# Attention masks and decay rows ahead of the wait for the keys, first row maxima ahead of the last level's queries, and the mixer turned by tile

## The chip, the cores and the metric

The kernel runs on one core of one Trainium2 chip. Its engines work side by side, each through its own queue in order: TensorE (PE in the profile; PEld is its weight load), VectorE (DVE), ScalarE (ACT), GpSimd (POOL) and SyncE (SP), which issues most of the transfers. They wait for each other by semaphores. The metric is the device time of one execution in microseconds; less is better.

## What is computed

A decoder trunk of two layers on 256 tokens of width 1024. In each layer one input projection feeds three groups of heads: a gated linear recurrence (HGRN2), an mLSTM, and a forgetting attention. Their outputs go through one output projection, and a channel mixer follows: dense in layer 0, eight experts of which each token takes two in layer 1. The parts that matter here, cut from the reference:

```python
def block(args):                      # forgetting attention, blocks of 128 queries, 8 heads
    qb, cb, bi = args
    qpos = bi * Q_BLOCK + jnp.arange(Q_BLOCK)
    s = (jnp.einsum('bhqd,bhkd->bhqk', qb, k).astype(f32) * scale
         + cb[..., None] - c[:, :, None, :])       # c = cumsum(log f): the decay rows
    s = jnp.where(kpos[None, :] <= qpos[:, None], s, -jnp.inf)
    p = jax.nn.softmax(s, axis=-1)
    return jnp.einsum('bhqk,bhkd->bhqd', p.astype(v.dtype), v)
...
for l in range(DEPTH):
    h = rmsnorm(x, attn_norm[l])
    ... = jnp.split(h @ w_in[l], split_idx, axis=-1)
    o_hg = hgrn2_mixer(...); o_ml = mlstm_mixer(...); o_fx = fox_mixer(...)
    mix = jnp.concatenate([o_hg, o_ml, o_fx], axis=-1)
    x = x + mix @ w_out[l]
    h = rmsnorm(x, ffn_norm[l])
    x = x + (swiglu(h, ...) if l % 2 == 0 else moe_swiglu(h, ...))
return rmsnorm(x, final_norm)
```

## The kernel before

**Products in halves.** A float32 operand is split in a high part (a cast, by ACT) and a low part (the rest, by DVE); three matmuls make one product (the helper `three`, L1664 to L1666). So each half slab of weights costs ACT one cast (`weights_high`, L887) and DVE one subtraction (`weights_low`, L1188) before PE can use it.

**The step loop.** The input projection is cut in 14 half slabs. PE, DVE and ACT each run a loop over 12 steps k with the same shape. In step k PE projects half slab k + 2 (`project`), and in the middle of it (`between`) multiplies one level of the HGRN2 scores (`level(l, k - 1)`, 9 levels) and turns attention weights. After the projection of step 3 PE spreads a row to 128 partitions with four products of 4 rows (L1896, eight matmuls in the profile). After that of steps 7, 8 and 9 it makes the attention scores of three groups (`attn_scores(l, 0..2)`); after that of steps 8 to 10 it turns the weights of a group (`attn_turn`), and from step 9 on it multiplies them with the values (`attn_apply`).

**Attention scores.** For each of two banks: one matmul that writes the causal mask (L1802), then per head one that adds the decay rows (L1807, from the tile `CT`), then per head queries by keys (L1813). `CT` holds the decay rows' high part, cast by ACT (L986, semaphore `s_cth`), and their low part, by DVE (L1393, `s_ctl`). Group 0 first waits for the mLSTM exponents to have left the banks (`s_e0`), for eight evacuated half slabs (`s_pe`; the keys are the last two of them), and for `s_ctl`. Groups 1 and 2 wait for the exponentials of the group before (`s_ex`), which read the same banks.

**DVE's step.** In step k: the level's queries (`level_queries`, L1229 and for level 8 L1232), the differences of the next level (`level_difference`, L1216 to L1222), in step 7 the decay rows' low part, in steps 8 to 10 the row maxima of a group (`attn_max`: two reductions L1257 and a negation L1261), then the copy of the last level's scores (`level_copy`), the attention weights (`attn_weights`), and the low part of half slab k + 4. ACT's step: the level's decays (L967, L969), the exponentials (`attn_exp`, L915), the copy of turned weights (L924), the evacuation (L871 for the values) and the cast of half slab k + 4. POOL makes the level's keys (L775).

**The end of the mixers.** After the loop PE makes the sums of the mLSTM and HGRN2 heads. Then come the output projection's rows that belong to attention (`for i in (NHALF, NHALF + 1)`, 48 matmuls of 512 columns), then the turns of the other heads' output `OM`, tile 0 into bank 3 and tile 1 into bank 0 (L1970), each after its wait for `s_og`. ACT copies each turned tile (L1014, `s_me`), DVE makes its low part (`mix_low`, L1199, `s_ml`), and PE goes on with the rows of these heads (L1977, L1978, L1983).

Of the kernel before, what the change touches and what calls it, by code (L numbers as in the profile page):

```python
# [21 lines left out]
P = 128  # L22
F32 = mybir.dt.float32
F32R = mybir.dt.float32r
I32 = mybir.dt.int32
ALU = mybir.AluOpType
# [8 lines left out]
def bass_hybrid_trunk_kernel(nc, x, attn_norm, w_in, hgrn_lb, hgrn_norm, mlstm_conv, mlstm_b_i,  # L35
# [3 lines left out]
    _, SEQ, D = x.shape  # L39
    DEPTH = w_in.shape[0]  # L40
    T = SEQ // P
# [5 lines left out]
    NFH = FW // DH  # L47
# [20 lines left out]
    NHALF = 2 * len(SLABS)  # L68
# [47 lines left out]
    with ExitStack() as ctx:  # L116
# [6 lines left out]
        ps = [ctx.enter_context(nc.psum_tensor(f"bank{i}", [P, BANK], F32)) for i in range(8)]  # L123
# [31 lines left out]
        OM = last_slot[:, 0:1024].rearrange("p (t h d) -> p t h d", t=T, h=2 * NH)  # L155
# [8 lines left out]
        CT = nc.alloc_sbuf_tensor_at("CT", [P, SEQ], F32R, offset=shared + 4 * decay_at)  # L164
# [21 lines left out]
        ident = sb("ident", [P, P])  # L186
# [122 lines left out]
        s_pe = sem("projection_evacuated")  # L309
# [16 lines left out]
        s_cth = sem("decay_rows_high")  # L326
        s_ctl = sem("decay_rows_low")
# [23 lines left out]
        s_og = sem("heads_gated")  # L351
        s_mt = sem("mix_turned")
# [795 lines left out]
        def _(dve):  # L1148
# [151 lines left out]
            for l in range(DEPTH):  # L1300
# [60 lines left out]
                level_difference(l, 1)  # L1361

                for k in range(STEPS):
                    if 1 <= k < LEVELS:
                        level_queries(l, k)
                        if k + 1 < LEVELS:
                            level_difference(l, k + 1)
                    if k == 1:
                        dve.wait_ge(s_aT, l + 1)
                        for t in range(T):  # L1370
                            v = slice(t * P, (t + 1) * P)
                            if t:
                                dve.wait_ge(s_g, T * l + t)
                            dve.tensor_tensor_scan(gT[:, v], ps[7][0:NH, 64 + t * P:64 + (t + 1) * P], MM[0:NH, P:2 * P],
                                                   0.0 if t == 0 else gT[:, t * P - 1:t * P], ALU.max, ALU.max).then_inc(s_g, 1)
                    if k == 4:
                        dve.wait_ge(s_gi, 2 * l + 1)
                        dve.wait_ge(s_a, 2 * l + 2)
                        dve.tensor_tensor(bb[:, :, :], bb[:, :, :], ps[7][:, 400:408].rearrange("p (t h) -> p t h", t=T),
                                          ALU.add).then_inc(s_m, 1)  # L1380
                    if k == 6:

                        dve.wait_ge(s_gi, 2 * l + 2)
                        dve.wait_ge(s_cv, 4 * CK * (l + 1))
                        for h in range(NH):
                            g = ps[4 + h // 2][:, (h % 2) * SEQ:(h % 2 + 1) * SEQ]
                            dve.scalar_tensor_tensor(out=E[:, h // 2, h % 2, 0:SEQ], in0=g, scalar=aa[:, 0, h:h + 1],
                                                     in1=MM[:, :], op0=ALU.add, op1=ALU.min).then_inc(s_e0, 1)
                            dve.scalar_tensor_tensor(out=E[:, h // 2, h % 2, SEQ:], in0=g[:, P:], scalar=aa[:, 1, h:h + 1],
                                                     in1=MM[:, 0:P], op0=ALU.add, op1=ALU.min).then_inc(s_e0, 1)  # L1390
                    if k == 7:
                        dve.wait_ge(s_cth, l + 1)
                        dve.tensor_tensor(CT[32:32 + NFH, :], ps[7][0:NFH, 0:SEQ], CT[0:NFH, :].bitcast(F32),  # L1393
                                          ALU.subtract).then_inc(s_ctl, 1)
                    if 8 <= k < 11:
                        attn_max(l, k - 8)
                    if l == 0 and k == 0:
                        dve.wait_ge(s_prT, 1)
                        dve.tensor_copy(PC[:, :], ps[6][:, 0:NROWS]).then_inc(s_pc, 1)
                        dve.wait_ge(s_pc, 1)  # L1400
                        dve.tensor_tensor(LB[:, 0, :], PCl[:, 1, :], PCl[:, 0, :], ALU.subtract).then_inc(s_lb, 1)
                    if l == 0 and k == 7:
                        dve.wait_ge(s_rw, 16)
                        dve.wait_ge(s_pc, 1)
                        dve.tensor_tensor(RW[:, :, :], RW[:, :, :], bc(PC[:, GAINS0:NROWS].unsqueeze(2), [P, KD, NE]),
                                          ALU.mult).then_inc(s_rwg, 1)
                    if l == 0 and k == 2:
                        gate_weights_low(1)
                        lower_bound()
                    if k == 0:  # L1410
                        level_copy(l, 0)
                    if 2 <= k <= LEVELS:
                        level_copy(l, k - 1)
                    if 2 <= k < 2 + CK:
                        convolve(l, k - 2)
                    if 8 <= k < 11:
                        attn_weights(l, k - 8)
                    if k + 4 <= NHALF:
                        weights_low(l, k + 4)
                    if k >= 9:  # L1420
                        attn_out_low(l, k - 9)

                dve.wait_ge(s_e, l + 1)
                for r, b0, v in ((0, 2, slice(0, SEQ)), (1, 4, slice(SEQ, SEQ + P))):
                    dve.wait_ge(s_qk, 2 * l + r + 1)
                    n = v.stop - v.start
# [234 lines left out]
        def _(pe):  # L1661
# [129 lines left out]
            def attn_scores(l, g):  # L1791

                if g == 0:
                    pe.wait_ge(s_e0, 8 * (l + 1))
                    pe.wait_ge(s_pe, NHALF * l + 8)
                    pe.wait_ge(s_ctl, l + 1)
                else:
                    pe.wait_ge(s_ex, 3 * l + g)
                heads = range(NFH) if g == 0 else range(4 * (g - 1), 4 * g)
                n, w, qt = (4, P, 0) if g == 0 else (2, SEQ, 1)  # L1800
                for p in range(2):
                    pe.matmul(ps[4 + p][:, :].rearrange("q (c s) -> q c s", c=n), identr[:, :],  # L1802
                              NM[:, 2 * P - w:].unsqueeze(1).to_broadcast([P, n, w]), start=True, stop=False,
                              skip_group_check=True)
                for h in heads:
                    at = (h // 2 * w) % BANK
                    pe.matmul(ps[4 + h % 2][:, at:at + w], PICK[:, h:h + 1].to_broadcast([P, P]), CT[:, 0:w],  # L1807
                              start=False, stop=False, skip_group_check=True)
                for h in heads:
                    p, c = h % 2, h // 2  # L1810
                    r = slice(DH * p, DH * p + DH)
                    at = (c * w) % BANK
                    ins = pe.matmul(ps[4 + p][:, at:at + w], FQ[r, c, qt * P:(qt + 1) * P], FK[r, c, 0:w],  # L1813
                                    start=False, stop=True, skip_group_check=True)
                ins.then_inc(s_S, 1)
# [42 lines left out]
            for l in range(DEPTH):  # L1858
# [16 lines left out]
                for k in range(STEPS):  # L1875
                    if k == 1:
                        pe.wait_ge(s_a, 2 * l + 2)
                        for t in range(T):
                            ins = pe.transpose(ps[7][0:NH, 64 + t * P:64 + (t + 1) * P], aa[:, t, :], ident[:, :])
# [9 lines left out]
                    if k == 3:  # L1889

                        pe.wait_ge(s_g, T * (l + 1))
                        for t in range(T):
                            ins = pe.transpose(ps[7][:, 400 + t * NH:400 + (t + 1) * NH], gT[:, t * P:(t + 1) * P], ident[0:NH, 0:NH])
# [20 lines left out]
                for h in range(NH):  # L1914
                    c, p = h // 2, h % 2
# [6 lines left out]
                for h in range(NH):  # L1922
                    c, p = h // 2, h % 2
# [5 lines left out]
                for h in range(NH):  # L1929
                    c, p = h // 2, h % 2  # L1930
# [18 lines left out]
                def out_rows(i):  # L1949

                    pe.wait_ge(s_wil, NCAST * l + i + 1)
                    return cast_places(i)

                for i in (NHALF, NHALF + 1):
                    wh, wl = out_rows(i)
                    for n in range(2):
                        for t in range(T):
                            for r in range(2):
                                k, v = 4 + 2 * (i - NHALF) + r, slice(t * P, (t + 1) * P)
                                w = slice(r * D + n * BANK, r * D + (n + 1) * BANK)  # L1960
                                ins = three(ps[4 + 2 * n + t][:, :], mxh[:, k, v], mxl[:, k, v], wh[:, w], wl[:, w],
                                            k == 4, False)
                    if i == NHALF:
                        ins.then_inc(s_wk, 1)
                for t in range(T):
                    pe.wait_ge(s_og, T * l + t + 1)
                    b = ps[3] if t == 0 else ps[0]
                    om = OM[:, t, :, :].rearrange("p h d -> p (h d)")
                    for c in range(4):
                        ins = pe.transpose(b[:, c * P:(c + 1) * P], om[:, c * P:(c + 1) * P], ident[:, :])  # L1970
                    ins.then_inc(s_mt, 1)
                wa, wb = out_rows(NHALF + 2), cast_places(NHALF + 3)
                pe.wait_ge(s_me, T * l + 1)
                for n in range(2):
# [216 lines left out]
```

## Time and profile before

| what | value |
|---|---|
| median of 3 runs | 1481.24 us (1481.13 to 1481.51) |
| the profiled execution | 1481.19 us, span 1479.4 us |
| busy PE / DVE / ACT / POOL | 1460.5 / 1176.3 / 971.2 / 122.6 us |
| mean granted clock of PE | 0.994 |
| read from HBM, written | 435.36 MB, 14.16 MB |

Times of rows are microseconds from the span's start. In a timeline row stand the start, the length of the group, the engine, the line, the operation, the tile written and the tiles read, the shapes, how many (x2), and in brackets how long the engine was idle before it and what ended that. Several instructions of one line in a row are merged to one group, and matmuls overlap, so a group's start plus its length can lie behind the next start. Layer 0's mixers take about the first 150 us, its dense mixer goes to about 350, layer 1's mixers to about 504, and the experts fill the rest.

### The profile page before, as it was taken

Reading aid. Unit: us, or ns where it says so; the run is one execution under the profiler, and the core shown is the slowest. Engines: PE = TensorE matmul, PEld = TensorE weight load, DVE = VectorE, ACT = ScalarE, POOL = GpSimd, SP = SyncE. Lnnn points to the kernel's source line nnn. Section 1 sums busy time; section 2 is a strip of 40 time slices with the busy share of each in tenths; the row PEclk is TensorE's granted clock in tenths of the full one; section 3 lists DMA queues with packets and bytes.
Section 4 is the critical chain, followed back from the end, with each engine's and each line's share of the span. In section 5 each row is a group of like instructions: output and inputs, shape, how many; then the busy total and the mean of one; then the engine's idle time right before and its main releaser. Section 6 shows DMA issues by size and latency. Waiting matters only on the chain.

```text
span 1479.4 us, 20868 instructions
## 1 busy us (share of the span) xinstructions
PE 1460.5 (99%) x7859; PEld 1240.9 (84%) x7859; DVE 1176.3 (80%) x931; ACT 971.2 (66%) x892; POOL 122.6 (8%) x137
## 2 busy tenths in 40 slices
PE   9999999999999999999999999999999999999997
PEld 8978899998988888888888888888888888888885
DVE  5776555455885788888888888888888888888897
ACT  4455444444646477777777777777777777777775
POOL 5212000000120280000000000000000000000200
PEclk9999999999999999999999999999999999999999
DMA  8633966553342499999999999999999999999993
GB/s 253 222 115 114 315 231 231 190 171 129 115 142 87 171 342 393 396 391 394 380 357 397 389 369 386 385 370 384 388 376 373 394 375 368 394 379 363 399 394 150
DMA packets 210284, 450.27 MB, mean 304 GB/s; under 512 B 12940, under 2 KB 37048, under 8 KB 210232
## 3 DMA queue, kind: packets, MB, share of 16 engines
q1 hardware_dynamic: 209080, 445.35, 82.5%
q0 software_dynamic: 1152, 4.19, 0.7%
q8 instruction: 37, 0.61, 0.2%
q14 instruction: 15, 0.12, 0.0%
HBM read 435.36 MB, written 14.16 MB: 304 GB/s over the span
## 4 chain that ended last, share of the span: by engine, by line
PE 95%; ACT 2%; DVE 1%; issue 1%; POOL 1%; DMA 0%; POOLq 0%; DVEq 0%; ACTq 0%
PE bank L1664 29%; PE bank L1666 28%; PE bank L1665 28%; PE bank L2099 2%; PE bank L1785 1%; ACT XN L826 1%; PE bank L1823 0%; PE bank L1852 0%; PE bank L1682 0%; PE bank L2087 0%; ACT XN L915 0%; PE bank L2077 0%; POOL st L648 0%; PE bank L1742 0%; DVE low L1182 0%
## 5 line engine op out<-in xcount | busy, mean ns | idle before, releaser
L1182 DVE TENSOR_TENSOR low<-raw,high 128x2048 fp32r<-128x2048 f32 x336 | 766.9, 2291 | 104.6 <-ACT high L1088 104.6
L1088 ACT CAST high<-raw 128x2048 fp32r<-128x2048 f32 x335 | 642.3, 1918 | 178.2 <-PE bank L1666 178.2
L1664 PE MATMUL bank<-high,xeh 128*128 128x512 f32 x896 | 353.6, 395 | 0.0
L1666 PE MATMUL bank<-high,xel 128*128 128x512 f32 x896 | 349.5, 390 | 0.0
L1665 PE MATMUL bank<-low,xeh 128*128 128x512 f32 x896 | 348.8, 389 | 0.0
L1666 PEld LDWEIGHTS bank<-high,xel 128*128 128x128 f32 x896 | 168.1, 188 | 35.8
L1665 PEld LDWEIGHTS bank<-low,xeh 128*128 128x128 f32 x896 | 168.4, 188 | 33.7
L1664 PEld LDWEIGHTS bank<-high,xeh 128*128 128x128 f32 x896 | 168.3, 188 | 33.8 <-DVE low L1182 0.3
L1664 PE MATMUL bank<-high,hdh 128*128 128x512 f32 x448 | 175.2, 391 | 0.4 <-DVE low L1182 0.4
L1666 PE MATMUL bank<-high,hdl 128*128 128x512 f32 x448 | 174.4, 389 | 0.0
L1665 PE MATMUL bank<-low,hdh 128*128 128x512 f32 x448 | 174.4, 389 | 0.0
L1188 DVE TENSOR_TENSOR winl<-ring,winh 128x2048 fp32r<-128x2048 f32 x34 | 81.6, 2399 | 29.6 <-ACT winh L887 29.5
L1664 PEld LDWEIGHTS bank<-high,hdh 128*128 128x128 f32 x448 | 84.1, 188 | 18.0 <-DVE low L1182 0.9
L1666 PEld LDWEIGHTS bank<-high,hdl 128*128 128x128 f32 x448 | 84.1, 188 | 17.6
L1665 PEld LDWEIGHTS bank<-low,hdh 128*128 128x128 f32 x448 | 84.1, 188 | 17.2
L1666 PE MATMUL bank<-dTh,gul 128*128 128x256 f32 x336 | 95.1, 283 | 0.0
L1665 PE MATMUL bank<-dTl,guh 128*128 128x256 f32 x336 | 95.1, 283 | 0.0
L1664 PE MATMUL bank<-dTh,guh 128*128 128x256 f32 x336 | 95.0, 283 | 0.0
L807 POOL DMA_INDIRECT gathered<-routed,backi x4 | 9.8, 2453 | 839.3 <-DVE backi L1598 838.4
L1480 DVE TENSOR_TENSOR dwl<-dring,dwh 128x1024 fp32r<-128x1024 f32 x22 | 26.9, 1225 | 61.6 <-ACT dwh L1049 61.6
L887 ACT CAST winh<-ring 128x2048 fp32r<-128x2048 f32 x34 | 64.9, 1908 | 12.3 <-PE bank L1666 10.8
L1664 PE MATMUL bank<-hTh,winh 128*128 128x256 f32 x224 | 65.8, 294 | 1.2 <-issue 1.2
(348 smaller groups left out, 1981.3 us busy)
## 6 DMA issues: line engine op xcount, KB each, us to landing
raw<-in_moe_w_gate_dram SPq DMA_DIRECT2D x112, 1024.0 KB, 8.0
raw<-in_moe_w_up_dram SPq DMA_DIRECT2D x112, 1024.0 KB, 8.5
raw<-in_moe_w_down_dram SPq DMA_DIRECT2D x112, 1024.0 KB, 8.0
ring<-in_w_in_dram SPq DMA_DIRECT2D x10, 2048.0 KB
dring<-in_dense_w_gate_dram SPq DMA_DIRECT2D x5, 2048.0 KB
dring<-in_dense_w_up_dram SPq DMA_DIRECT2D x5, 2048.0 KB
dring<-in_dense_w_down_dram SPq DMA_DIRECT2D x5, 2048.0 KB
ring<-in_w_in_dram SPq DMA_DIRECT2D x8, 1024.0 KB, 9.0
```

The costliest lines, as they stand in the source:

```text
L807: pool.indirect_dma_start(gathered[:, c, t, :], None, routed.rearrange("b p d -> (b p) d"), bass.IndirectOffsetOnAxis(ap=backi[:, c, t:t + ...
L826: act.activation(XN[:, t, v], X[:, t, v], ACT.Square, scale=D ** -0.5, accum_out=st[:, i, 2 * n, t:t + 1]).then_inc(s_ss, 1)
L887: act.copy(cast_places(i)[0], half_unit(l, i)).then_inc(s_wih, 1)
L1088: act.copy(high[:, q % SPLIT, :], raw[:, q % RAW, :]).then_inc(s_hi, 1)
L1182: dve.tensor_tensor(low[:, q % SPLIT, :], raw[:, q % RAW, :], high[:, q % SPLIT, :].bitcast(F32), ALU.subtract).then_inc(s_lo, 1)
L1188: dve.tensor_tensor(wl, half_unit(l, i), wh.bitcast(F32), ALU.subtract).then_inc(s_wil, 1)
L1480: dve.tensor_tensor(dwl[:, i % 2, :], block_weights(i)[2], dwh[:, i % 2, :].bitcast(F32), ALU.subtract).then_inc(s_dwl, 1)
L1664: pe.matmul(o, xh, wh, start=first, stop=False)
L1665: pe.matmul(o, xh, wl, start=False, stop=False)
L1666: return pe.matmul(o, xl, wh, start=False, stop=last)
L1785: ins = pe.matmul(ps[2 + p][:, w], kk[r, v], q[r, w], start=True, stop=True)
L2099: ins = pe.transpose(ps[6][:, b * P:(b + 1) * P], hid[:, c % 2, b * P:(b + 1) * P], ident[:, :])
```

## The change

DVE's step loop: the low part of the decay rows moves from behind the queries and differences of step 7 to the front of that step, and the row maxima of group 0 move to the front of step 8. PE's scores of group 0: the waits for `s_pe` and `s_ctl` move behind the masks, and the one for `s_pe` behind the decay rows as well. PE's end of the mixers: the turn of tile 0 goes ahead of the last six matmuls of attention's rows; that of tile 1 stays.

```diff
@@ DVE's loop over the steps
                 for k in range(STEPS):
+                    if k == 7:
+                        dve.wait_ge(s_cth, l + 1)
+                        dve.tensor_tensor(CT[32:32 + NFH, :], ps[7][0:NFH, 0:SEQ], CT[0:NFH, :].bitcast(F32),
+                                          ALU.subtract).then_inc(s_ctl, 1)
+                    if k == 8:
+                        attn_max(l, 0)
                     if 1 <= k < LEVELS:
                         level_queries(l, k)
...
-                    if k == 7:
-                        dve.wait_ge(s_cth, l + 1)
-                        dve.tensor_tensor(CT[32:32 + NFH, :], ps[7][0:NFH, 0:SEQ], CT[0:NFH, :].bitcast(F32),
-                                          ALU.subtract).then_inc(s_ctl, 1)
-                    if 8 <= k < 11:
+                    if 9 <= k < 11:
                         attn_max(l, k - 8)
@@ PE, attn_scores
                 if g == 0:
                     pe.wait_ge(s_e0, 8 * (l + 1))
-                    pe.wait_ge(s_pe, NHALF * l + 8)
-                    pe.wait_ge(s_ctl, l + 1)
...
+                if g == 0:
+                    pe.wait_ge(s_ctl, l + 1)
                 for h in heads:
...
+                if g == 0:
+                    pe.wait_ge(s_pe, NHALF * l + 8)
                 for h in heads:
                     p, c = h % 2, h // 2
@@ PE, the end of the mixers
+                def turn_mix(t):
+
+                    pe.wait_ge(s_og, T * l + t + 1)
+                    b = ps[3] if t == 0 else ps[0]
+                    om = OM[:, t, :, :].rearrange("p h d -> p (h d)")
+                    for c in range(4):
+                        ins = pe.transpose(b[:, c * P:(c + 1) * P], om[:, c * P:(c + 1) * P], ident[:, :])
+                    ins.then_inc(s_mt, 1)
+
                 for i in (NHALF, NHALF + 1):
                     wh, wl = out_rows(i)
                     for n in range(2):
                         for t in range(T):
+                            if (i, n, t) == (NHALF + 1, 1, 1):
+                                turn_mix(0)
                             for r in range(2):
...
-                for t in range(T):
-                    pe.wait_ge(s_og, T * l + t + 1)
-                    b = ps[3] if t == 0 else ps[0]
-                    om = OM[:, t, :, :].rearrange("p h d -> p (h d)")
-                    for c in range(4):
-                        ins = pe.transpose(b[:, c * P:(c + 1) * P], om[:, c * P:(c + 1) * P], ident[:, :])
-                    ins.then_inc(s_mt, 1)
+                turn_mix(1)
```

## Rows read from the trace of the kernel before

**Rows 1.** The page's part 4, shares by engine of the chain that ended last.
```profile
PE 95%; ACT 2%; DVE 1%; issue 1%; POOL 1%; DMA 0%; POOLq 0%; DVEq 0%; ACTq 0%
```

**Rows 2.** Waits of PE, whole span: us in total, times, longest us.
```profile
PE bank L1802 <- ACT attention L871: 1.4, 2, 0.7
...
PE bank L1802 <- ACT XN L915: 1.0, 2, 0.5
...
PE bank L1977 <- ACT mxh L1014: 0.7, 2, 0.3
```

**Rows 3.** Timeline of PE, layer 0: start us, us, line, operation, idle before.
```profile
89.12 0.39 PE L1666 MATMUL bank<-winh,hTl 128*128 128x512 f32 x1
90.21 0.70 PE L1802 MATMUL bank<-NM,identr 128*128 128x512 f32 x2 [0.70 <-ACT attention L871]
...
91.68 1.16 PE L1813 MATMUL bank<-attention 64*128 64x128 f32 x16
...
95.41 0.39 PE L1666 MATMUL bank<-winh,hTl 128*128 128x512 f32 x1
95.72 1.16 PE L1785 MATMUL bank<-QD,KDk 64*128 64x64 f32 x16
...
99.45 0.39 PE L1666 MATMUL bank<-winh,hTl 128*128 128x512 f32 x1
100.34 0.73 PE L1802 MATMUL bank<-NM,identr 128*128 128x512 f32 x2 [0.50 <-ACT XN L915]
```

**Rows 4.** Timeline of DVE, layer 0.
```profile
84.96 2.28 DVE L1188 TENSOR_TENSOR winl<-ring,winh 128x2048 fp32r<-128x2048 f32 x1
87.56 0.43 DVE L1229 TENSOR_TENSOR QD<-HQ,DX 128x256 f32<-128x256 f32 x1 [0.31 <-ACT DX L969]
...
89.65 0.41 DVE L1393 TENSOR_TENSOR CT<-bank,CT 8x256 fp32r<-8x256 f32 x1
...
91.96 2.29 DVE L1188 TENSOR_TENSOR winl<-ring,winh 128x2048 fp32r<-128x2048 f32 x1 [0.95 <-ACT winh L887]
94.17 1.78 DVE L1232 TENSOR_TENSOR QD<-HQ,DX 128x512 f32<-128x512 f32 x1
95.88 1.27 DVE L1257 TENSOR_REDUCE nmx<-bank 128x4 f32<-128x512 f32 x2
```

**Rows 5.** Timeline of ACT, layer 0.
```profile
84.60 0.35 ACT L986 CAST CT<-bank 8x256 fp32r<-8x256 f32 x1
...
97.39 0.37 ACT L915 ACTIVATE XN<-bank,nmx 128x128 f32<-128x128 f32 x1 [4.26 <-DVE nmx L1261]
```

**Rows 6.** Timelines of POOL (first and last row) and DVE (between), layer 0.
```profile
93.20 2.20 POOL L775 TENSOR_TENSOR KDk<-HK,DX 128x512 f32<-128x512 f32 x1 [4.07 <-ACT DX L969]
...
130.44 1.94 DVE L1428 SCALAR_TENSOR_TENSOR ER<-bank,ER 128x512 f32<-128x512 f32 x4
...
131.21 0.63 POOL L778 TENSOR_SCALAR G<-G 128x512 f32<-128x512 f32 x1 [35.80 <-ACT G L999]
```

**Rows 7.** Timelines of DVE (first row) and PE, end of layer 0's mixers.
```profile
141.42 0.69 DVE L1451 TENSOR_TENSOR attention<-attention,G 128x512 f32<-128x512 f32 x1
...
146.43 1.04 PE L1970 MATMUL bank<-ident,attention 128*128 128x128 f32 x8
147.79 0.47 PE L1977 MATMUL bank<-hTh,mxh 128*128 128x512 f32 x1 [0.33 <-ACT mxh L1014]
```

**Rows 8.** Chain that ended last, layers 0 and 1: start us, us, what.
```profile
58.91 1.83 PE bank L1896 x8
63.80 1.09 PE bank L1785 x16
...
402.40 1.83 PE bank L1896 x8
408.78 1.09 PE bank L1785 x16
```

**Rows 9.** PE by stretch, layer 1: us, busy, granted clock, DMA share, GB/s.
```profile
406.00:408.00 2.00, 2.00 (x11) 0.50 0.02 3
```

## The prediction

> **What bounds the kernel now.** I read the shares of the chain that ended last first: TensorE (PE) holds 95% of it [rows 1]. So a change is worth what it takes out of PE's own line, plus what it takes out of the few links where PE stands still. Then I read PE's waits over the whole span [rows 2]. Three of them lie where the diff works, and each comes twice, once for each layer: 0.70 us before the first attention scores, 0.50 us before the second scores, 0.33 us before the first mixer rows of the output projection. That is 1.53 us a layer, 3.06 us in all: the gain can't be much larger, unless the clock moves with it. Last I read the timelines of PE, DVE, ACT and POOL around the three places of layer 0 [rows 3 to 7].
>
> A wait's modelled idle is a little less than what it costs, since matmuls overlap. Without a wait the step from one matmul's start to that of another kind is 0.31 us (95.41 to 95.72) where the record of the first is 0.39 us long [rows 3]: 0.08 us of overlap is lost at each wait. So the three waits cost 0.78, 0.58 and 0.41 us.
>
> **First wait, 0.78 us a layer.** The page puts it down to ACT's copy L871, which ends at 90.13. But the scores wait for eight evacuations, and that copy is the tenth; the source is to be held against the name. What they do wait for is the low part of the decay rows: DVE's L1393, 89.65 to 90.06 [rows 4], and PE starts at 90.21 [rows 3]. That instruction stood behind the queries and differences of a level. In the changed order it stands in front of them. Its own input, the high part by ACT, is done at 84.95 [rows 5]; DVE gets free of the weights at 87.24 [rows 4]; so it runs at about 87.25 to 87.65, and PE comes at 89.43. The wait goes, with 1.8 us to spare. The cost: the queries of level 7 start 0.1 us later (0.41 us, of which 0.31 us was idle before them [rows 4]); PE wants them at 95.72 [rows 3]. POOL's work on the keys takes its turn earlier or later there, and the next DVE instruction on weights idles 0.95 us before 91.96 [rows 4]; that absorbs it. Cost nothing; with the cover gone 0.1 us.
>
> The masks (2 matmuls, inside the 0.70 us group) and decay rows are also put ahead of the waits. They are the same instructions with the same waits among them, in another order. With the decay rows early, no wait is left for them to fill, so I take zero for it. Bounds: nothing, and at most the same 0.78 us, which is counted once.
>
> **Second wait, 0.58 us a layer.** Back from PE: the second scores need the exponentials of the first, which ACT starts at 97.39 after 4.26 us idle, on the negated maxima [rows 5]. Those follow the two reductions at 95.88, which follow the queries of level 8 (94.17, 1.78 us long), which follow the weights that end at 94.25 [rows 4]. The scores are done at 92.84 [rows 3], so the reductions, put first, can start at 94.17. All of it moves by 95.88 less 94.17, 1.71 us: the exponentials end at about 98.6 and not 100.3. PE, 0.78 us earlier by the first part, comes at 99.45 + 0.31 - 0.78 = 98.98. The wait goes, with 0.35 us to spare, the tightest margin in this sum. What is queued behind the reductions on DVE: the queries of level 8, the copy of level 7, the attention weights. The queries then end at about 97.5; level 8 is multiplied after half of the next projection, over 6 us later. The attention weights wait for the exponentials and come 1.7 us earlier. Cost nothing.
>
> The 1.78 us of those queries is mostly a wait for POOL: POOL's L775 stands from 93.20 to 95.40 [rows 6], and the same kind of instruction at half the width took 0.43 us when it came first [rows 4]. Would the reductions be held too? They read one tensor, from the banks. The nearest rows are DVE's L1428, which reads a bank and one tile: four took 1.94 us, 0.48 each, while POOL's L778 worked beside them from 131.21 to 131.84 [rows 6]. They were not held, so I take no hold.
>
> The Trainium skill says so too (SBUF — State Buffer, Who interferes with whom): on this chip a tensor_reduce never contends with GpSimd, while an instruction with two SBUF inputs does. By it the sum stays as it is; no reduction here lies beside POOL, so no row shows it.
>
> **Third wait, 0.33 us a layer net.** Eight transposes run from 146.43, ACT copies the first four's bank only after them, and PE idles 0.33 us [rows 7]. In the change the first four go ahead of the last six matmuls of the rows before. Those six take 6 x 0.23 = 1.4 us, more than the copy and its latency, so the wait goes: 0.41 us. It costs one more change of kind, after the first four: a first matmul is 0.47 us [rows 7] where others are 0.39 us [rows 3], 0.08 us. The first tile is needed at 146.43 - 1.4 = 145.05 and was ready at 142.11 [rows 7]: 2.9 us to spare, and both hang on the same earlier end of the projections, so they move together. The mixer's multiplications, their low parts and the out-projection's weights are on DVE behind that and keep their distance to PE.
>
> **DMA.** No transfer and no place in SP's or POOL's queue is moved. Loads are released by DVE's and PE's counts and come earlier with them.
>
> **Sum.** 0.78 + 0.58 + 0.33 = 1.69 us a layer, 3.4 us in all. By idle alone, with the switch paid: 0.70 + 0.50 + 0.33 - 0.08 = 1.45, 2.9 us. With the switch free: 1.77, 3.5 us. The profiled execution took 1481.19 us (span 1479.4), the median is 1481.24 us, so there is nothing to correct: 1477.8 us, 1477.7 to 1478.3 for this case alone. Behind each place the chain is PE again, so nothing fixed in time stands there to give the gain back.
>
> **The rivals.**
>
> *The clock moves with the shift.* In layer 1 the granted clock falls to 0.50, 1.2 GHz, between about 404.6 and 408.2 [rows 9], after eight matmuls that use 4 rows (L1896). From their start to the next level is 4.89 us in layer 0 and 6.38 us in layer 1 [rows 8]: the fall costs 1.49 us. Layer 0 has the same instructions and no fall, so it hangs on when they come. Layer 1 will come 1.69 us earlier. If its fall goes: 3.4 + 1.5, 1476.3 us. If one more comes somewhere behind: 3.4 - 1.5, 1479.3 us. For the first: two tries of the same code, one fall. Against both: the three runs lie within 0.38 us, so places don't change by themselves.
>
> The Trainium skill has the clock gate's judging run free of the kernel (TensorE: Matmul & The Clock Gate, What's actually happening). By that the fall would come or go between executions, 1.5 us apart; the runs' spread does not show it.
>
> *The reductions are held by POOL.* They start at 95.40, the exponentials end at 99.8, and PE, there at 98.98, waits 0.85 us. The layer then gains 0.48 us for the first two and 0.33 us for the third: 1.6 us in all, 1479.6 us. Rows 6 speak against it.
>
> *The gain is given back behind the mixers*, by a load that doesn't come earlier: layer 0's part is lost before the dense mixer, 1.7 us are left, 1479.5 us. No wait of PE on a transfer is among its waits, which speaks against it.
>
> *Slower: PE stops for the first tile of the heads.* The wait for it now stands in front of six matmuls. It decides when the tile comes more than 2.9 us later against PE; above that each us costs one in each layer. To be 3 us slower in all it has to be 6.1 us late, by a held DVE or POOL chain: 1484.3 us. Nothing in the change lengthens that chain.
>
> **How the numbers follow.** What a measurement of this kernel can tell from no change is about 0.2%, 3.0 us; the forecast lies just beyond. Chances: the sum as worked out 0.45 (of it 0.38 beyond 3.0 us), layer 1's fall gone 0.25, one fall more 0.12, held reductions 0.08, given back 0.07, slower 0.03. Faster: 0.38 + 0.24 and a little for falls that move elsewhere, 0.64; slower 0.04; within 0.2%: 0.32. The range reaches from the fall gone, with the upper sum (1476.2) and 0.4 us for the clock of later stages, to one fall more or a given-back layer: 1475.8 to 1479.5.
>
> **What would show it.** Right: PE's waits at L1802 are gone in both layers and L1977 starts without idle; the decay rows' low part runs right behind the weights at about 87.3; ACT's first exponential comes at about 95.7; layer 1's second level stands 1.7 us earlier. A wait left at the second L1802, with reductions that start at POOL's end, is the second rival. A granted clock that is full over all of layer 1's first levels is the first. Wrong would be a new wait at L1970's first four, or PE's waits gone and the span as before.

## The result and the profile after

In five executions beside five of the kernel before the changed kernel took 1474.50 us in the median (1473.47 to 1474.93) against 1481.13 us (1479.92 to 1481.51): ratio 0.9962, 95% interval 0.9951 to 0.9974. Two later comparisons, e5 and e10 below, gave 0.9967 (0.9955 to 0.9978) and 0.9968 (0.9956 to 0.9980). Over all executions of this study the medians are 1480.4 us (77 of the kernel before) and 1474.8 us (18 of the changed one). The forecast was 1477.8 us, with a range from 1475.8 to 1479.5 us: right in sign, but 3.4 us less where 6.6 us less were measured, about half, and the median lies below the range.

The page of the changed kernel: its span, the busy times, and the shares by engine of the chain that ended last.

```profile
span 1473.1 us, 20866 instructions
...
PE 1458.1 (99%) x7859; PEld 1240.0 (84%) x7859; DVE 1172.5 (80%) x931; ACT 971.7 (66%) x892; POOL 122.9 (8%) x137
...
PE 97%; DVE 1%; ACT 1%; issue 1%; POOL 0%; DMA 0%; SPq 0%; POOLq 0%; DVEq 0%; ACTq 0%
```

PE's share of the chain went from 95% [rows 1] to 97%. These are the four longest of PE's waits over the whole span; the three of [rows 2] are gone from the list.

```profile
PE bank L1673 <- POOL mhalf L718: 1.9, 1, 1.9
PE bank L1684 <- DVE XN L1157: 1.4, 3, 0.6
PE bank L1666 <- issue: 1.2, 2, 0.6
PE bank L2043 <- issue: 0.7, 1, 0.7
```

PE's timeline at the attention scores of layer 0, which answers to [rows 3]. The scores' last group is L1817 now.

```profile
87.44 0.39 PE L1668 MATMUL bank<-winh,hTl 128*128 128x512 f32 x1
87.66 0.61 PE L1802 MATMUL bank<-NM,identr 128*128 128x512 f32 x2
88.11 1.00 PE L1809 MATMUL bank<-CT,PICK 128*128 128x128 f32 x8
89.05 1.16 PE L1817 MATMUL bank<-attention 64*128 64x128 f32 x16
...
96.83 0.39 PE L1668 MATMUL bank<-winh,hTl 128*128 128x512 f32 x1
97.06 0.64 PE L1802 MATMUL bank<-NM,identr 128*128 128x512 f32 x2
97.53 0.63 PE L1809 MATMUL bank<-CT,PICK 128*128 128x256 f32 x4
98.09 1.14 PE L1817 MATMUL bank<-attention 64*128 64x256 f32 x8
```

The kernel before has these rows behind its masks, beside those of [rows 3]:

```profile
90.75 1.00 PE L1807 MATMUL bank<-CT,PICK 128*128 128x128 f32 x8
...
100.91 0.62 PE L1807 MATMUL bank<-CT,PICK 128*128 128x256 f32 x4
101.47 1.13 PE L1813 MATMUL bank<-attention 64*128 64x256 f32 x8
```

No bracket is left at L1802. From the last projection matmul to the keys' products it is 89.05 - 87.44 = 1.61 us, where it was 91.68 - 89.12 = 2.56 us [rows 3]: 0.95 us saved. For the second scores it is 98.09 - 96.83 = 1.26 us; the kernel before took 101.47 - 99.45 = 2.02 us: 0.76 us saved. The step from a projection matmul to a mask is 0.22 to 0.23 us when nothing is waited for.

DVE, POOL and ACT over the same stretch; ACT's rows are the first and the last part of the exponentials.

```profile
85.59 0.41 DVE L1366 TENSOR_TENSOR CT<-bank,CT 8x256 fp32r<-8x256 f32 x1
86.03 1.46 DVE L1229 TENSOR_TENSOR QD<-HQ,DX 128x256 f32<-128x256 f32 x1
...
92.49 1.28 DVE L1257 TENSOR_REDUCE nmx<-bank 128x4 f32<-128x512 f32 x2
93.81 0.17 DVE L1261 TENSOR_SCALAR nmx<-nmx 128x8 f32<-128x8 f32 x1
93.89 0.69 DVE L1232 TENSOR_TENSOR QD<-HQ,DX 128x512 f32<-128x512 f32 x1
```

```profile
91.52 2.19 POOL L775 TENSOR_TENSOR KDk<-HK,DX 128x512 f32<-128x512 f32 x1 [4.31 <-ACT DX L969]
```

```profile
94.02 0.37 ACT L915 ACTIVATE XN<-bank,nmx 128x128 f32<-128x128 f32 x1 [2.57 <-DVE nmx L1261]
...
96.68 0.24 ACT L915 ACTIVATION_READ_ACCUMULATOR XN<-bank,nmx 128x1 f32 x1
```

The decay rows' low part comes right behind the weights, the reductions right behind the next ones. All of this profile stands 1.67 us earlier from level 0 on, ahead of every edit (39.46 and 37.79 us, explained below). With 1.67 us added the low part starts at 87.26 and the first exponential at 95.69, where the prediction has about 87.3 and 95.7. The two reductions take 1.28 us with POOL at work from 91.52 to 93.71 beside them, as they took 1.27 us alone [rows 4]: they are not held. The queries behind them, which start as POOL ends, take 0.69 us where they took 1.78 us [rows 4]. The queries of level 7 now run beside POOL's work on the keys (85.92 to 87.21) and take 1.46 us where they took 0.43 us [rows 4]; the difference behind them takes 0.41 us where it took 1.52 us (L1221), so this costs nothing. The exponentials end at 96.92, and PE starts at 97.06: the margin that the prediction put at 0.35 us is 0.14 us, since PE comes earlier than it said.

The end of the mixers, to be read against [rows 7]. The first block is the changed kernel, the second the kernel before: its matmul seven steps ahead of the turns, and further on eight transposes with a matmul behind them that waits for nothing.

```profile
141.41 0.39 PE L1668 MATMUL bank<-winh,mxl 128*128 128x512 f32 x1
141.65 0.60 PE L1964 MATMUL bank<-ident,attention 128*128 128x128 f32 x4
142.00 0.48 PE L1666 MATMUL bank<-winh,mxh 128*128 128x512 f32 x1
142.31 0.39 PE L1667 MATMUL bank<-winl,mxh 128*128 128x512 f32 x1
...
143.48 0.60 PE L1964 MATMUL bank<-ident,attention 128*128 128x128 f32 x4
143.83 0.48 PE L1986 MATMUL bank<-hTh,mxh 128*128 128x512 f32 x1
```

```profile
144.80 0.39 PE L1666 MATMUL bank<-winh,mxl 128*128 128x512 f32 x1
...
158.98 1.04 PE L1682 MATMUL bank<-ident,XN 128*128 128x128 f32 x8
...
159.77 2.52 PE L1671 MATMUL bank<-identr 128*128 128x512 f32 x10
```

From 141.41 to the next rows at 143.83 it is 2.42 us; before, from the matmul at 144.80 to 147.79, it was 2.99 us: 0.57 us saved. Four transposes take 0.35 us to the next start, the change of kind costs 0.08 us (0.31 us at 142.00 where others take 0.23 us).

The clock in layer 1, against [rows 9]. The eight small matmuls start at 398.33 here (402.26 before), and it is full behind them.

```profile
400.00:402.00 2.00, 2.00 (x16) 1.00 0.00 0
402.00:404.00 2.00, 2.00 (x24) 1.00 0.00 0
```

### The profile page after: what moved, and what is told of

Its sections match the earlier page's. It is cut to its first block, busy times and chain, and to the rows that moved or that the text cites. A ratio compares the mean times of both kernels' runs of the same rounds, so it can differ in the third digit from the quotient of the medians.

```text
span 1473.1 us, 20866 instructions
## 1 busy us (share of the span) xinstructions
PE 1458.1 (99%) x7859; PEld 1240.0 (84%) x7859; DVE 1172.5 (80%) x931; ACT 971.7 (66%) x892; POOL 122.9 (8%) x137
## 4 chain that ended last, share of the span: by engine, by line
PE 97%; DVE 1%; ACT 1%; issue 1%; POOL 0%; DMA 0%; SPq 0%; POOLq 0%; DVEq 0%; ACTq 0%
PE bank L1666 29%; PE bank L1668 29%; PE bank L1667 29%; PE bank L2108 2%; PE bank L1787 1%; PE bank L1827 0%; PE bank L1817 0%; PE bank L1856 0%; PE bank L1684 0%; PE bank L2096 0%; DMA gain<-in_attn_norm_dram 0%; PE bank L2086 0%; ACT XN L826 0%; PE bank L1837 0%; DVE low L1182 0%
```

## The experiments

Medians alone don't settle these differences: the 31 executions of the kernel before that stand beside e1 to e4 lie between 1478.24 and 1481.68 us. So each profile is also cut at the same landmarks. The first column is the step from level 0's product to the first product of weights and values (layer 0 / layer 1), which holds both waits at the scores; the second goes on to the dense mixer (layer 0) or to the last transposes (layer 1) and holds the turns; the third goes from there to the first expert matmul, the last to the end of the span. Apart from that end, all are starts on PE's timeline.

| kernel | to the values' product | to the mixers' end | routing | to the end |
|---|---|---|---|---|
| before | 70.40 / 71.89 | 54.81 / 49.12 | 14.96 | 960.49 |
| changed | 68.68 / 68.73 | 54.25 / 48.55 | 16.24 | 960.57 |
| e1, decay rows | 70.41 / 70.41 | 54.81 / 49.12 | 16.44 | 960.63 |
| e2, maxima | 69.62 / 71.12 | 54.82 / 49.12 | 16.23 | 960.57 |
| e3, turn | 71.86 / 70.41 | 54.25 / 48.55 | 14.88 | 960.64 |
| e4, masks | 70.42 / 70.40 | 54.81 / 49.12 | 15.28 | 960.58 |
| e5, changed again | 68.69 / 68.71 | 54.24 / 48.55 | 14.85 | 960.55 |
| e6, without the masks' part | 68.69 / 68.69 | 54.24 / 48.56 | 16.22 | 960.54 |
| e7, small matmuls spread, before | 70.80 / 70.81 | 54.81 / 49.12 | 14.86 | 960.61 |
| e8, the same, changed | 69.07 / 69.04 | 54.24 / 48.56 | 16.22 | 960.60 |
| e9, scores' parts | 68.72 / 68.72 | 54.82 / 49.14 | 16.21 | 960.50 |
| e10, changed, third | 68.72 / 68.73 | 54.24 / 48.55 | 16.24 | 960.54 |
| e11, router filled | 68.73 / 68.73 | 54.23 / 48.55 | 19.23 | 960.57 |
| e12, longer cover | 68.72 / 68.72 | 54.24 / 48.55 | 17.06 | 960.65 |

In the first two columns a step repeats within 0.05 us from execution to execution where the clock is full. That is the measure for what follows; a figure there that stands out by 1.5 us has a clock fall in it. The routing column is never without half clock. The last one repeats within 0.2 us.

**e1: only the decay rows' low part.** e1 to e4 were run beside 31 executions of the kernel before, median 1480.18 us.

```diff
                 for k in range(STEPS):
+                    if k == 7:
+                        dve.wait_ge(s_cth, l + 1)
+                        dve.tensor_tensor(CT[32:32 + NFH, :], ...).then_inc(s_ctl, 1)
                     if 1 <= k < LEVELS:
                         level_queries(l, k)
...
-                    if k == 7:
-                        dve.wait_ge(s_cth, l + 1)
-                        dve.tensor_tensor(CT[32:32 + NFH, :], ...).then_inc(s_ctl, 1)
```

> Only the low part of the decay rows goes to the front of step 7. Theory A (each wait costs what the two profiles show from start to start): the first wait goes, 0.95 us a layer or a little less; but the second wait grows by as much, since the exponentials stay where they are, so PE is held until the same 100.3 us: the kernel gains nothing, 1481 us within 0.5 us. Theory B (the three edits' gains add up one by one): 1.9 us less, 1479.2 us. Theory C (much of the measured gain is TensorE's clock, which falls to half in other places once layer 1 comes at another time): with no shift of layer 1, the fall at 404.6 us stays as in the kernel before.

Median 1480.47 us, ratio 0.9998 (0.9989 to 1.0008). PE's timeline:

```profile
88.95 0.39 PE L1666 MATMUL bank<-winh,hTl 128*128 128x512 f32 x1
89.18 0.61 PE L1802 MATMUL bank<-NM,identr 128*128 128x512 f32 x2
...
98.34 0.39 PE L1666 MATMUL bank<-winh,hTl 128*128 128x512 f32 x1
100.17 0.73 PE L1802 MATMUL bank<-NM,identr 128*128 128x512 f32 x2 [1.44 <-ACT XN L915]
```

The first wait is gone, and the second is 1.44 us where it was 0.50 us [rows 3]. It took over all of the gain: the step stays at 70.41 us. Theory A holds, the gains do not add up one by one. No fall came in either layer, so that part of theory C, that without a shift the fall stays where it is, is wrong.

**e2: only the row maxima.**

```diff
+                    if k == 8:
+                        attn_max(l, 0)
                     if 1 <= k < LEVELS:
                         level_queries(l, k)
...
-                    if 8 <= k < 11:
+                    if 9 <= k < 11:
                         attn_max(l, k - 8)
```

> Only group 0's row maxima go to the front of step 8. Theory A: the first wait stays (0.70 us idle), the second goes: 0.76 us a layer, 1.5 us in all, 1479.6 us by waits alone. Theory C: layer 1 comes 0.76 us earlier, and its clock fall at 404.6 us may go, which would add up to 1.5 us: 1478.1 us. If POOL held the reductions, the second wait would stay at a third of a microsecond or more.

Median 1479.11 us, ratio 0.9992 (0.9982 to 1.0001), which the medians can't tell from no change. PE's timeline:

```profile
89.11 0.39 PE L1668 MATMUL bank<-winh,hTl 128*128 128x512 f32 x1
90.19 0.70 PE L1804 MATMUL bank<-NM,identr 128*128 128x512 f32 x2 [0.70 <-ACT attention L871]
...
99.44 0.39 PE L1668 MATMUL bank<-winh,hTl 128*128 128x512 f32 x1
99.66 0.61 PE L1804 MATMUL bank<-NM,identr 128*128 128x512 f32 x2
```

The first wait stays at 0.70 us, the second is gone: 70.40 less 69.62, 0.78 us in layer 0. In layer 1 the step is 71.12, that is 0.77 us less than 71.89: both have a fall in them.

**e3: only the turn of tile 0** (the third part of the diff).

> Only the turn of tile 0 goes ahead of the last six matmuls. Theory A: 0.57 us a layer, 1.1 us in all, 1480.0 us; both waits at the scores stay at 0.70 and 0.50 us. The prediction's term was 0.33 us a layer, 0.7 us in all. Theory C: layer 1 comes 0.57 us earlier; if its clock fall goes, 1478.5 us.

Median 1479.36 us, ratio 0.9997 (0.9987 to 1.0006), which the medians can't tell from no change. The landmarks can: 54.25 and 48.55 us where the kernel before has 54.81 and 49.12, 0.57 us a layer. PE's waits at the scores are as in [rows 2]:

```profile
PE bank L1802 <- ACT attention L871: 1.4, 2, 0.7
...
PE bank L1802 <- ACT XN L915: 1.0, 2, 0.5
```

This profile has its fall in layer 0, where the kernel before had none, behind the same L1896:

```profile
60.00:62.00 2.00, 2.00 (x13) 0.54 0.00 0
62.00:64.00 2.00, 2.00 (x17) 0.61 0.52 117
```

It costs 71.86 - 70.40 = 1.46 us. Nothing in this kernel differs from the one before up to that point.

**e4: only the masks and decay rows ahead of the waits** (the second part of the diff).

> Only PE's own order in the scores of group 0: masks ahead of the wait for the decay rows, and these ahead of the wait for the keys. Theory A: the masks (0.45 to 0.54 us) fill part of the first wait, but the second wait holds PE to the same time as before (100.3 us), so nothing in the time, 1481 us within 0.5 us. A theory in which the masks' place is a gain of its own: 0.9 to 1.1 us less.

Median 1479.70 us, ratio 1.0001 (0.9991 to 1.0010). PE's timeline:

```profile
88.78 0.39 PE L1666 MATMUL bank<-winh,hTl 128*128 128x512 f32 x1
89.01 0.61 PE L1800 MATMUL bank<-NM,identr 128*128 128x512 f32 x2
89.77 1.11 PE L1807 MATMUL bank<-CT,PICK 128*128 128x128 f32 x8 [0.15 <-DVE CT L1393]
...
98.57 0.39 PE L1666 MATMUL bank<-winh,hTl 128*128 128x512 f32 x1
100.00 0.73 PE L1800 MATMUL bank<-NM,identr 128*128 128x512 f32 x2 [1.04 <-ACT XN L915]
```

The masks run at once, the decay rows wait 0.15 us, and the second wait is 1.04 us: again it takes over what the first gave. Nothing in the time.

**e5 and e10: the changed kernel again.**

> The changed kernel once more, for more executions of both kernels on one chip. Executions of the kernel before spread over 3.4 us (1478.2 to 1481.7), since TensorE's clock falls to half in other places from one to the next. Theory A (the three waits are all of it): 4.6 us less than the kernel before between medians and between lowest values, so a median near 1475.6 us, and the 6.6 us of the first ten executions was partly the draw of the falls. Theory C (the change also moves the falls for good): 6 us or more again.

> The changed kernel once more on this chip. Theory A: 4.6 us less than the kernel before, ratio 0.9969. With ten more executions the medians should come nearer to that than the 6.6 us of the first ones.

e5: median 1474.66 us (1473.31 to 1476.28) against 1479.84, 5.2 us less. e10: 1476.56 us (1473.19 to 1477.31) against 1480.84, 4.3 us less. The lowest of all executions are 1473.19 and 1477.97 us, 4.8 us apart. That is nearer to theory A's 4.6 us than to 6 us or more. Each of the two intervals still holds 6 us. The means of all executions are 5.2 us apart, and from the spread of the 77 and 18 executions I estimate a 95% interval of 4.5 to 5.8 us for that, which leaves 6 us out.

**e6: the changed kernel without the masks' part.**

```diff
                 if g == 0:
                     pe.wait_ge(s_e0, 8 * (l + 1))
+                    pe.wait_ge(s_pe, NHALF * l + 8)
+                    pe.wait_ge(s_ctl, l + 1)
```

and the two later waits are left out.

> The changed kernel, but PE's waits for the keys and the decay rows back ahead of the masks. Theory A: the decay rows are ready 1.8 us before PE comes, so the place of the waits is worth nothing: same as the changed kernel within 0.3 us, and no idle at L1802. Rival: the waits between the groups of matmuls have a price or a gain of their own, 0.1 us or more a layer in the steps from start to start.

Median 1474.74 us in five executions, and 68.69 us in both layers: the same as the changed kernel within 0.05 us. The masks' place is worth nothing once the decay rows are early.

**e9: the three parts at the scores together,** without the turn.

> The three edits at the attention scores without the turn by tile. Alone, the decay rows and the masks gave nothing, and the maxima one wait. Theory A: together both waits go, 1.71 us a layer (2.56 + 2.02 us from the last projection matmul to the keys' products before, 1.61 + 1.26 us after), 3.4 us in all: 1476.7 us where the kernel before has 1480.1 us. Theory B (the edits' gains add up one by one, from what each showed alone): 1.5 us less. The idle of 0.33 us at L1977 stays.

Median 1477.57 us against 1480.84, ratio 0.9979 (0.9970 to 0.9988), 3.3 us less. The landmark is 68.72 us in both layers: 1.68 us a layer, where e1, e2 and e4 alone gave 0, 0.78 and 0. With e3's 0.57 us it makes up the changed kernel's steps. Theory B's 1.5 us (ratio 0.9990) lies just outside the interval, and the steps exclude it.

**e7 and e8: the four products of 4 rows in two places,** in the kernel before and in the changed one.

```diff
-                        for h in range(NH):
+                    if k in (3, 4):
+                        for h in (0, 1) if k == 3 else (2, 3):
                             ins = pe.matmul(ps[4 + h // 2][...], SEL[:, h, :], gT[:, :], start=True, stop=True)
-                        ins.then_inc(s_gi, 1)
+                        if k == 4:
+                            ins.then_inc(s_gi, 1)
```

> The kernel before, with the four products of 4 rows (L1896) cut in two pairs, one after the projection of step 3 and one after that of step 4. Theory of the clock: the falls in layers 0 and 1 come after this stretch of small matmuls; with 0.9 us in two places they don't come any more: no profile shows one near 60 or 405 us, the executions spread less, and the median falls by 0.5 to 1.5 us, to about 1479. Rival: the falls come from elsewhere (the levels, the turns), and the median stays at that of the kernel before.

> The changed kernel with the four products of 4 rows cut in two pairs in the same way. Theory of the clock: less by as much as the same edit takes from the kernel before, 0.5 to 1.5 us, so about 1474.5 us and the fastest of all. Rival: same as the changed kernel.

e7: median 1479.18 us, ratio 0.9995 (0.9986 to 1.0004). e8: 1476.89 us, ratio 0.9978 (0.9969 to 0.9987), and with that 2.2 us behind e5, which ran beside it; 0.7 us of these are in the steps. The two profiles differ by 1.4 us more at the start (39.02 and 37.65 us at level 0's product) and by 1.4 us at the routing, both by the clock; the medians' difference beyond 0.7 us can't be assigned from one profile each. The edit costs 0.35 to 0.4 us a layer in changes of kind (70.80 for 70.40, 69.07 for 68.69). No fall stands in the layers of these two profiles, but neither does one in most others, so it isn't shown that the edit keeps them out. The forecast of a gain was wrong.

**e11 and e12: more work around the router.** e11 puts a matmul of 512 columns, whose result isn't used, behind every second of the router's first six products of a tile; e12 sets the matmuls that cover the wait for the choice to eight.

```diff
                                     start=(k == 0), stop=(k == KD - 1))
+                    if k % 2 and k < KD - 1:
+                        keep_running(0, 1)
```

```diff
-    GAP_NORM, GAP_DENSE, GAP_CHOICE = 10, 6, 4
+    GAP_NORM, GAP_DENSE, GAP_CHOICE = 10, 6, 8
```

> The changed kernel with six matmuls of 512 columns put between the router's products (32 matmuls of 8 columns each), whose result is not used. They cost about 6 x 0.25 us and some changes of kind, 2 us, on the path. Theory of the clock: the fall that comes with the router's stretch of small matmuls gets rarer or shorter; the gather behind it takes 5.4 to 5.9 us at half clock. If it goes altogether, some 2 to 3 us come back, and the kernel is at 1474 us, 1 us less than the changed one, or the same. Rival: the fall stays, and the kernel is 2 us slower.

> The changed kernel with eight instead of four matmuls of 512 columns behind the router's products, where PE waits for DVE's choice of the experts. At full clock four more take 0.9 us and fit the wait; at half clock they take 1.7 us and hold the choice back by some 1.5 us. Theory of the clock: as the fall is there already, they end it at best one step earlier; 0.5 to 1.5 us slower. Rival: the gather runs at the full clock, 2 us less.

e11: median 1476.41 us in six executions, e12: 1475.93 us in six, e10 beside them 1476.56 us in six. The medians don't tell them apart. In the profiles the routing step is 19.23 and 17.06 us against 16.24 us, and the clock is at half through most of it in each: the added work is paid in the profiles, and the fall stays. No version is faster than the changed kernel by more than the executions spread.

## Why the prediction fell short

**The places and the mechanism were right.** All three waits went, for the reasons given: the first on the decay rows and not on the copy that the page names (e4 shows it, where its name now is DVE's L1393), the second because the reductions start 1.7 us earlier, the third since the copy runs beside six matmuls. The masks are worth zero (e6), POOL doesn't hold the reductions, no load gives the gain back (from the dense mixer's first product to level 0 of layer 1 it is 218.3 us in every profile), no new wait came.

**The price of a wait was mis-sized: the terms 0.78, 0.58 and 0.33 us measured 0.95, 0.76 and 0.57 us.** Together 1.69 us a layer was forecast; the landmarks give 1.70 us at the scores and 0.57 us at the turns, 2.27 us a layer and 4.54 us in all for 3.4. The failing step is "0.08 us of overlap is lost at each wait". That overlap was read from the change to a level's product, which takes 0.31 us. The change to a mask takes 0.22 to 0.23 us, so 0.16 us of overlap is lost; and the two masks after a wait take 0.54 us to the next line (90.21 to 90.75), where unhindered ones take 0.45 us (87.66 to 88.11). 0.70 + 0.16 + 0.09 is the 0.95 us. The second wait adds up in the same way: 0.50 + 0.16 + 0.10 us, the last term from 0.57 and 0.47 us. The kernel before showed the overlap too, in the step from one projection matmul to the next, 0.23 us at a record of 0.39 us.

At the turns the record of four transposes is 0.60 us long and the next matmul starts after 0.35 us: 0.25 us of overlap, not 0.08, and 0.33 + 0.25 us is the gain within 0.01 us. The 0.08 us that the prediction took off for one more change of kind is there, but it is given back: eight transposes in a row take 0.79 us to the next start (158.98 to 159.77), twice four take 0.70 us. So the prediction's bound by idle, "the gain can't be much larger" than 3.06 us, was wrong as well.

**The rest is TensorE's clock, and not by the rival's mechanism.** The profiled pair differs by 6.3 us: 4.54 us by the waits, 1.67 us by a fall at the start of the kernel, which is in one profile and not in the other (level 0's product at 39.46 and 37.79 us, ahead of every edit), 1.49 us for the fall in layer 1, less 1.28 us for a longer stretch at half clock at the routing, and 0.1 us behind it. The rival said that layer 1's fall hangs on when layer 1 comes. e1 and e4 left it within 0.4 us of where it was and had none, e2 moved it and had one, e3 had it in layer 0, ahead of every edit. And the three profiles of the changed kernel itself differ: one of them, e10, has the fall at the start, and e5 has a shorter one at the routing. So falls change from one execution to the next.

The prediction set this aside with the words "the three runs lie within 0.38 us, so places don't change by themselves". That was the second failing step: 31 executions lie within 3.4 us. The Trainium skill has the clock gate's judging run free of the kernel (TensorE: Matmul & The Clock Gate, What's actually happening). The three profiles of the changed kernel agree with that; three equal times were too few to speak against it.

**What stays open.** Over all executions the medians are 5.5 us apart and the means 5.2 us (4.5 to 5.8), the landmarks account for 4.5 us. None of the eight profiles without PE's waits at the scores has a fall in the layers, three of the six with waits have one; but e3's stands at 60 us, ahead of the waits. At the routing it is the other way: seven of the eight without waits have a stretch at half clock of 10 us or more, two of the six with waits. Whether the change moves the falls at all is not shown; fourteen profiles don't decide it.

## What to carry to other kernels

A wait costs more than the idle before it: compare start to start with the same change of kind where nothing is waited for, or add the overlap of the record before it (at the scores 0.09 us more came from slower masks behind the wait). Waits in a row pay as one: removing the first alone gave nothing, since the next took it over, and both together gave more than twice what the second gave alone. And when a few tenths of a percent matter, cut the profile at landmarks: steps repeat within 0.05 us where the 77 executions of one kernel spread over 3.8 us.

## What the runs showed of the hardware

TensorE's granted clock fell from 1.00 to 0.50 at three kinds of places while PE worked: at the start (ten of fourteen profiles; level 0's product stands at 39.0 to 39.5 us with it, at 37.7 to 38.1 us without), behind the matmuls of 4 rows (three profiles, 1.46 to 1.50 us), and at the routing, in every profile, for about 7 or 10 us and once (e11) for 14. A fourth fall, in every profile too, comes behind PE's last matmul and costs it nothing. These rows are the router's products and the gather of e5, and then the same of the first profile of the changed kernel; the kernels are the same:

```profile
498.26 3.71 PE L1837 MATMUL bank<-RW,tokens_results 128*128 128x8 f32 x32
...
505.70 5.41 PE L2086 MATMUL bank<-selS,XN 128*128 128x128 f32 x32 [0.19 <-DVE selS L1514]
```

```profile
498.46 4.72 PE L1837 MATMUL bank<-RW,tokens_results 128*128 128x8 f32 x32
...
506.92 5.85 PE L2086 MATMUL bank<-selS,XN 128*128 128x128 f32 x32 [0.19 <-DVE selS L1514]
```

The clock is at half from 502.0 to 509.0 us in the first and from 500.8 to 511.0 us in the second: the first one's products ran at the full clock (3.71 us), the second one's only in part (4.72 us), and its gather stood longer at half clock (5.85 for 5.41 us).
